# The order of projection and states on TensorE in the rounds ahead of the scan loop of a hybrid S5 / attention / mixture-of-experts backbone

## What is computed

```
proj = concat(h_ctx, h_lat) @ w_in
u, qa, ka, va, qn, kn, vn, gates = split(proj)
bu = einsum('blgh,gph->blgp', u, b_bar)          # 32 groups of 16 channels, 64 states, two directions
_, states = associative_scan(_recurrence_combine, (a, bu), axis=1)
```

## Time and profile before

| what | value |
|---|---|
| time before, median of 3 runs | 1774.99 us (1772.9 to 1782.16) |
| the profiled execution | 1786.03 us, its span 1784.4 us |
| PE busy | 1662.3 us, 93% of the span |
| DVE, ACT, POOL busy | 787.0, 464.5, 302.4 us |
| mean granted TensorE clock | 0.957 of full speed |
| rounds of layer 0 | 75.8 to 149.4 us of the span |
| rounds of layer 1 | 1089.4 to 1165.9 us of the span |

### The profile page before, as it was taken

One profiled execution on the slowest core, in us unless ns is written; L12 is line 12 of the kernel. 1 busy time (PEld: TensorE's weight loads), 2 busy tenths in 40 slices (PEclk: granted clock), 3 DMA queues, 4 the chain that ended last, 5 costly groups with the idle time before them and its releaser, 6 DMA issues.

```text
span 1784.4 us, 39455 instructions
## 1 busy us (share of the span) xinstructions
PE 1662.3 (93%) x15972; PEld 1059.0 (59%) x15972; DVE 787.0 (44%) x1901; ACT 464.5 (26%) x1025; POOL 302.4 (17%) x296
## 2 busy tenths in 40 slices
PE   5999998889999999999999988999798999899996
PEld 2467555554444444477777756676556888655653
DVE  3578864660110111544444468688656111423222
ACT  4011212552000000344444450111035000333332
POOL 0004341880000000201111120044347000000000
PEclk9999998999999999999999998998679999999997
DMA  9410459509211153389999864115580346799995
GB/s 390 132 68 24 136 224 342 102 1 359 112 71 71 71 213 117 157 288 389 391 384 392 326 265 119 47 53 198 193 195 25 129 171 258 275 396 416 406 405 232
DMA packets 106729, 381.20 MB, mean 214 GB/s; under 512 B 40784, under 2 KB 60496, under 8 KB 68752
## 3 DMA queue, kind: packets, MB, share of 16 engines
q1 hardware_dynamic: 86832, 335.45, 50.4%
q0 software_dynamic: 5648, 33.16, 5.4%
q10 hardware_dynamic: 14128, 10.85, 2.3%
HBM read 360.55 MB, written 29.36 MB: 219 GB/s over the span
## 4 chain that ended last, share of the span: by engine, by line
PE 74%; DVE 8%; DMA 6%; POOL 4%; issue 3%; ACT 2%; SPq 2%; ACTq 0%; DVEq 0%; POOLq 0%
PE tile_ps L708 61%; PE out_ps L708 6%; PE turn_ps L708 5%; POOL arena L2257 3%; SPq L596 2%; DMA h<-in_wpack 2%; DMA vn<-in_wpack 2%; PE turn_ps L1039 1%; DVE arena L2076 1%; DMA x<-in_xT 1%; DMA ring<-in_wpack 1%; DVE arena L2168 1%; DVE smx L2058 1%; ACT arena L1526 1%; PE tile_ps L933 0%
## 5 line engine op out<-in xcount | busy, mean ns | idle before, releaser
L708 PE MATMUL tile_ps<-h,ring 128*128 128x512 f32 (+1 forms) x1312 | 478.2, 520 | 4.1 <-ACT h L1292 3.8
L708 PEld LDWEIGHTS tile_ps<-h,ring 128*128 128x128 f32 x1312 | 254.8, 195 | 211.0 <-issue 193.5
L708 PE MATMUL tile_ps<-arena,ring 128*128 128x512 f32 (+1 forms) x704 | 235.3, 486 | 2.4 <-issue 2.4
L708 PEld LDWEIGHTS tile_ps<-arena,ring 128*128 128x128 f32 x704 | 133.6, 190 | 95.3 <-issue 86.3
L708 PE MATMUL tile_ps<-arena 128*32 128x256 f32 (+2 forms) x2896 | 164.4, 336 | 9.3 <-DMA arena<-u_scratch 4.0
L2257 POOL TENSOR_SCALAR arena<-arena,smx 128x512 f32<-128x512 f32 (+1 forms) x96 | 129.1, 1363 | 71.2 <-DVE smx L2064 70.7
L708 PEld LDWEIGHTS tile_ps<-arena 128*32 128x32 f32 (+1 forms) x2896 | 112.8, 119 | 45.4 <-issue 10.6
L1498 ACT ACTIVATE arena<-tile_ps 128x512 f32<-128x512 f32 (+1 forms) x56 | 27.5, 491 | 347.3 <-PE tile_ps L708 347.3
L2098 DVE TENSOR_TENSOR arena<-tile_ps,arena 128x512 f32<-128x512 f32 (+1 forms) x32 | 17.9, 558 | 212.2 <-PE tile_ps L708 212.2
L708 PE MATMUL out_ps<-arena 64*128 64x64 f32 (+2 forms) x1032 | 95.9, 350 | 11.0 <-issue 10.7
L708 PEld LDWEIGHTS out_ps<-arena 64*128 64x128 f32 (+2 forms) x1032 | 76.9, 216 | 18.8 <-issue 18.1
(11 more groups left out here) (367 smaller groups left out, 2293.4 us busy)
## 6 DMA issues: line engine op xcount, KB each, us to landing
ring<-in_wpack SPq DMA_DIRECT2D x176, 1024.0 KB, 8.6
arena<-in_wpack SPq DMA_DIRECT2D x58, 1024.0 KB, 15.4
h<-in_wpack SPq DMA_DIRECT2D x14, 1024.0 KB, 20.5
qa<-in_wpack SPq DMA_DIRECT2D x11, 1024.0 KB, 15.4
qn<-in_wpack SPq DMA_DIRECT2D x11, 1024.0 KB, 17.0
kn<-in_wpack SPq DMA_DIRECT2D x11, 1024.0 KB, 18.6
vn<-in_wpack SPq DMA_DIRECT2D x11, 1024.0 KB, 20.0
arena<-sorted_in POOLq DMA_DIRECT2D x19, 256.0 KB, 8.5
```

What stands on the lines that cost most here:

```text
L708: return nc.tensor.matmul(out, lhsT, rhs, start=start, stop=stop)
```

## The change

In rounds 1 to 6, TensorE now does the projection ahead of the states: turned weights of q, projection, states of q - 1. Round 0 (no states), round 7 (no projection) and round 8 read as before. The list of jobs, from which the banks follow, is changed alike. No engine but TensorE has its instructions in another order.

```
--- before.py
+++ after.py
@@ -237,8 +237,8 @@
         names.append(fill[0])
         for q in range(NQ + 1):
             names += [(l, "wt", q, 0), (l, "wt", q, 1)] if q < NQ else []
+            names += fill[1 + q:2 + q] if q < NQ - 1 else []
             names += [(l, "st", q - 1)] if q else []
-            names += fill[1 + q:2 + q] if q < NQ - 1 else []
@@ -933,6 +933,8 @@
                                 ins = nc.tensor.transpose(bank(job)[:, g * P:(g + 1) * P],
                                                           wm[:, r, g].rearrange("p h j -> p (h j)"), c("ident"))
                             full(job, ins)
+                    for job in fill[1 + q:2 + q] if q < NQ - 1 else []:
+                        projection(job, c0)
                     if q:
                         o = q - 1
                         job = (l, "st", o)
@@ -945,8 +947,6 @@
                                 ins = mm(bank(job)[:, (r * GQ + g) * NCH:(r * GQ + g + 1) * NCH], wt[:, r, g, :],
                                          ug[:, o * GQ + g, :])
                         full(job, ins)
-                    if q < NQ - 1:
-                        projection(fill[1 + q], c0)
```

## The result

The changed kernel takes 1787.12 us in the median of 20 runs, before 1779.55 us in 20 runs beside them. The ratio is 1.0059 with a 95% interval of 1.0034 to 1.0085, so it is slower by 6 to 15 us. The profiled execution has a span of 1788.0 us.

A forecast was written before the change was run, and what follows sets the result against it. TensorE, holding 74% of the chain, was taken to bound the kernel. Layer costs of 7.7 and 1.8 us plus clock terms 3.4, 3.4 and -1.7 gave 14.6, added to 1775 for about 1789 us; range 1778 to 1803.

The forecast's parts named there:

- Cost 1, the boundary: Ahead of rounds 2 to 7 in each layer, ScalarE's copies wait for the states and hold TensorE: 1.18 us each.
- Cost 2, VectorE in round 3: Layer 0: VectorE's later work readies round 3's turned weights at 106.49, TensorE idles 2.74 us; round 4 starts 3.02 us later.
- Layer 0 without any fall: Layer 0 with no new drop to the lower clock: 3.02 us plus four boundaries of 1.18, +7.7 us.
- Gain in layer 1: Projection covers the `ug` wait, round 4 starts 3.0 us earlier; four boundaries give back 4.7, so +1.8 us.
- The clock: TensorE's clock may drop behind new gaps: +3.4 us for layer 0's 2.74 us gap, +3.4 at plain boundaries, -1.7 at last states.
- one fall of ten: Of the ten plain boundaries, one is followed by the lower clock: +3.4 us.
- The term for the last states: Layer 0's existing drop of the clock ahead of the last states may go or stay: -1.7 us.
- The second rival: The clock falls at most boundaries, six of ten: 33 us added, 1808 us; chance 0.12.
- the rule of the Trainium skill: Short idles between matmul groups while PSUM banks are cycled can swing the clock between two levels; spoke against the change.
- Swallowed delay: Rival: a weight-load wait of 10.55 us in layer 0's scan loop absorbs the 7.7 us; about 1775 us, chance 0.07.
- Cheap boundary: Rival: copies are seen earlier, boundaries cost 0.3 us, layer 1 keeps its 3.0 us; about 1775 us, chance 0.03.
- The clock that stays full: Rival: no fall at layer 0's new gaps, and the old fall there goes too; +6.1 us, 1781 us, chance 0.17.

The follow-up runs named there:

- The second buffer: The changed kernel with a second buffer for the turned weights, so ScalarE's copies wait for the states two rounds back; ratio 0.9979 against before.
- both cures: The changed kernel plus a second buffer for the turned weights and carry_powers split over rounds 4 to 6; ratios 0.9913 and 0.9868 against before.
- the two cures: On the old order: a second buffer for the turned weights and carry_powers moved to rounds 4 to 6; ratio 0.9958 against before.

## Why the prediction was right, step by step

**Cost 1, the boundary: right.** Forecast 1.18 us, measured 1.10. The profile shows the gap as 0.82 us and not 1.1, as it counts idle time from the end of the states' last record, 0.16 us past the point where they give way. The pattern ahead of the last states gave it; the transposes began 0.98 us after the states gave way (91.19 + 1.74 = 92.93 to 93.91), 0.11 earlier than the forecast's 1.09. The second buffer shows the cause.

**Cost 2, VectorE in round 3: right.** Forecast at 106.49, measured 106.38, from a start 0.06 us earlier. The gap of 2.66 us was forecast at 2.74. Layer 0 without any fall was forecast at +7.7 us, and the kernel changed in layer 0 alone has +7.4.

**Gain in layer 1: right.** Forecast idle times 0.7 and 6.2 us, measured 0.84 and 6.22; forecast +1.8 for the stretch, measured +1.4. The second profile of this order, of the kernel changed in layer 1 alone, has -0.2, so +1.4 is one of two results. (By the prediction's own terms, the projection of round 2 starts at 1101.69 + 2.05 = 1103.74 and not 1103.70; 0.04 us changes nothing.)

**The clock: right in kind, the terms off.** A fall behind the long wait came in both layers; it cost 2.9 us in layer 0 (0.89 on the transposes, 1.98 on the projection) where 3.4 stood, and it does not come each time, as the kernel changed in layer 0 alone shows. The term "one fall of ten" at the plain boundaries (+3.4) was wrong: of 42 gaps of 0.82 us in five profiles (10, 12, 10, 5 and 5) none was followed by a fall. The term for the last states (-1.7) went the other way in this profile: both layers fell there. Over the seven profiles with that gap of 1.42 us in both layers (before among them), it fell in 7 of 14. The second rival, a fall at most boundaries, and the rule of the Trainium skill weighed there ("TensorE: Matmul & The Clock Gate", section "A second HAM failure mode: psum-queue depth-cycling") thus did not hold for these gaps. They stand behind a projection of 3.5 to 7.2 us and the states; at rounds 2 to 6 a projection follows the transposes, at round 7 the states do.

**The sum.** Forecast 14.6 us. Measured from the first turned weights to the first `vn` product, so with the last states: layer 0 from 73.64 (75.77 to 149.41) to 83.67 us (75.71 to 159.38), layer 1 from 76.45 (1089.43 to 1165.88) to 79.12 (1097.29 to 1176.41). That is 10.0 + 2.7 = 12.7 us. The medians are 7.6 us apart, and the ratio gives 10.5, with 6 to 15 for its interval. Both sums lie in it, 14.6 near its upper end.

**What was luck.** Two terms of the clock, +3.4 and -1.7, did not come true, and together they put 1.7 us into the sum for nothing. And the forecast of 1789 us is so near the measured 1787.12 because two misses offset each other: the base of 1775 us, from three runs, was 4.6 us below the 1779.55 us of 20 runs, and the added 14.6 us was 4.1 more than the 10.5 of the ratio.

**Why the two spans differ by 3.6 us only** (1788.0 less 1784.4). Behind layer 1's rounds, from the first `vn` product to the piece of 610 products behind layer 1's scan loop, the profile after has a shorter piece than before. The rows are of TensorE alone, before first:

```profile
1165.88:1375.84 209.96, 189.46 (x1527) 0.85 0.45 136
```

```profile
1176.41:1379.94 203.53, 181.22 (x1526) 0.89 0.46 140
```

6.4 us with nothing changed there, and the clock at 0.89 against 0.85. Between layer 0's piece of 610 products and layer 1's rounds it is another 2.6 us (685.65 us from 403.78, and 683.10 from 414.19), with the clock at 0.99 and 1.00. This is no gift of the change. The new order with both cures, one and the same kernel in two profiles, on two chips, differs more in the piece behind layer 1's rounds:

```profile
1144.94:1357.26 212.32, 189.75 (x1527) 0.85 0.45 134
```

```profile
1137.05:1338.43 201.38, 179.29 (x1527) 0.90 0.47 142
```

10.9 us, with the clock at 0.85 and 0.90. One chip shows such a spread too: 35 executions of before on the chip of the first experiments took 1770.65 us (mean clock 0.970) to 1800.83 us (0.949), the slower ones at the lower clock nearly throughout. So one execution can hide, or double, a change of this size, and I read the cost in the stretch.

**The rivals.** Swallowed delay: falls, by the 10.4 us at 414.19 in layer 0. Cheap boundary: falls, by 1.10 us. The clock that stays full: half true, as it did so at the plain gaps but not behind the wait of round 3, nor ahead of the last states.

## What to carry to other kernels

Before an instruction is moved later, list every in-order engine whose next work waits for it, also for a reason other than its result: here ScalarE waited for the states only in order to overwrite their input. A copy that was hidden under a projection of 6.9 us came onto the path and cost 1.1 us each round. The wait that a reorder covers is kept only if the engines that feed the next step can keep up: the reorder lost 0.6% alone, and with a second buffer and VectorE's long piece moved away it was 0.9 to 1.3% ahead of before, of which 0.4% is what the two cures gave the old order.

## What the runs showed of the hardware that I had not expected

The granted clock behind a short gap of TensorE is no fixed matter. Behind gaps of 0.82 us the clock fell in 0 of 42 cases, behind gaps of 1.42 us with 64-column products on both sides in 7 of 14, and 2.66 us in one of two; the four longer ones of the new order (3.81, 6.22, 6.22 and 7.24 us) all did. The same instructions behind layer 1's rounds took 212.32 us in one profile and 201.38 in another, on another chip, with the clock at 0.85 and 0.90. On a single chip, 35 executions of one kernel spread over 30 us, and the time went with the mean clock (1770.65 us at 0.970, 1800.83 us at 0.949).
